# Banded attention scores from fp16 high and low parts, a later partial sum in each group, and other orders in two head loops

## The reference

```python
s = jnp.einsum('bnqhgd,bnkhd->bnhgqk', qb, kc).astype(jnp.float32) * (HEAD_DIM ** -0.5)
s = jnp.where(mask[None, :, None, None], s, NEG_INF)
p = sink_softmax(s, sinks).astype(v.dtype)
o = jnp.einsum('bnhgqk,bnkhd->bnqhgd', p, vc)
```

## Time and profile before

| | |
|---|---|
| median of 3 runs | 1790.39 us |
| profiled execution | 1791.63 us, of it 1790.0 us between first and last instruction |
| TensorE (PE) busy | 1734.6 us, 97% of the span |
| VectorE (DVE) busy | 1061.5 us, 59% |
| ScalarE (ACT) busy | 876.1 us, 49% |
| GpSimd (POOL) busy | 226.5 us, 13% |

### The profile page before, as it was taken

The page is one execution under the profiler, slowest core; times in us unless marked ns, Lnnn a source line. Parts: engine busy times, 40 slices in busy tenths (PEclk is TensorE's granted clock), DMA queues, the critical chain, the costliest instruction groups (busy, mean ns, idle before and its releaser), DMA issues.

```text
span 1790.0 us, 36899 instructions
## 1 busy us (share of the span) xinstructions
PE 1734.6 (97%) x14593; PEld 1356.9 (76%) x14593; DVE 1061.5 (59%) x2267; ACT 876.1 (49%) x1345; POOL 226.5 (13%) x313
## 2 busy tenths in 40 slices
PE   6999999999999999999999999999999999999996
PEld 4888876787677867786667777777777777778885
DVE  6634646574557546774766875555665666574343
ACT  7545542553345444553335664544655555464442
POOL 1410010111011001101105102011011100011110
PEclk8999999999999999999999999999999999999998
DMA  9523323552255225642455533233233323234432
GB/s 305 154 71 97 81 54 95 168 162 77 60 174 169 71 63 180 197 142 76 131 161 168 171 95 100 80 94 91 70 82 82 82 71 81 77 95 129 114 96 100
DMA packets 270549, 204.51 MB, mean 114 GB/s; under 512 B 8116, under 2 KB 254080, under 8 KB 269136
## 3 DMA queue, kind: packets, MB, share of 16 engines
q1 hardware_dynamic: 251200, 131.71, 26.7%
q0 software_dynamic: 19232, 71.13, 11.7%
HBM read 168.05 MB, written 38.80 MB: 116 GB/s over the span
## 4 chain that ended last, share of the span: by engine, by line
PE 81%; DVE 8%; ACT 5%; issue 3%; DMA 2%; SPq 0%; ACTq 0%; DVEq 0%; POOL 0%; POOLq 0%
PE PP L604 53%; PE PP L853 7%; PE PP L633 3%; PE BS L697 2%; PE BS L507 2%; PE B L1050 2%; PE BS L757 2%; PE B L728 2%; ACT W L1229 1%; PE B L507 1%; ACT AR L1602 1%; DVE W L1836 1%; PE PP L1143 1%; PE B L779 1%; DMA W<-in_w_out_a 1%
## 5 line engine op out<-in xcount | busy, mean ns | idle before, releaser
L604 PE MATMUL PP<-H,W 128*128 128x280 f16 (+1 forms) x8640 | 1053.4, 281 | 2.6 <-DVE W L1836 1.9
L604 PEld LDWEIGHTS PP<-H,W 128*128 128x128 f16 x8640 | 833.4, 98 | 189.6 <-issue 21.3
L1229 ACT ACTIVATE W<-W,SCL 128x1024 f16<-128x1024 f32 x240 | 262.6, 1138 | 312.3 <-DVE SCL L1767 271.5
L1836 DVE SCALAR_TENSOR_TENSOR W<-W,SCL 128x1024 f16<-128x1024 f32 x240 | 310.4, 1303 | 131.1 <-ACT W L1229 126.6
L1218 ACT ACTIVATE wjunk<-W 128x2048 bf16<-128x2048 f32 x120 | 227.7, 1898 | 16.4 <-DMA W<-in_w_out_a 12.0
L853 PE MATMUL PP<-O,W 128*128 128x280 f16 x1536 | 189.1, 283 | 4.1 <-DVE H L2094 2.7
L853 PEld LDWEIGHTS PP<-O,W 128*128 128x128 f16 x1536 | 147.4, 98 | 43.9 <-issue 8.5
L1602 ACT ACTIVATE AR<-AR 128x128 f32<-128x128 f32 x136 | 53.0, 391 | 90.6 <-DVE AR L2381 90.6
L604 PE MATMUL PP<-O,W 128*128 128x280 f16 x576 | 69.6, 283 | 0.5 <-DVE AR L2321 0.5
L2011 DVE SCALAR_TENSOR_TENSOR AR<-AR,B 128x512 f32<-128x512 f32 x32 | 23.9, 747 | 73.2 <-PE B L728 51.2
L1766 DVE TENSOR_SCALAR step<-PP 128x1 int32<-128x1 int32 x107 | 16.5, 154 | 83.8 <-PE PP L534 81.0
(11 more groups left out here) (352 smaller groups left out, 1861.7 us busy)
## 6 DMA issues: line engine op xcount, KB each, us to landing
W<-in_w_in_a SPq DMA_DIRECT2D x48, 1024.0 KB, 6.0
W<-in_w_in_b SPq DMA_DIRECT2D x32, 1024.0 KB, 6.0
out<-AR POOLq DMA_DIRECT2D x36, 512.0 KB, 4.3
AR<-in_state_gla POOLq DMA_DIRECT2D x32, 512.0 KB, 6.6
W<-in_w_out_b SPq DMA_DIRECT2D x16, 1024.0 KB, 6.1
W<-in_w_out_a SPq DMA_DIRECT2D x16, 512.0 KB, 5.3
W<-in_w_out_a SPq DMA_DIRECT2D x32, 256.0 KB, 3.9
W<-in_w_kv SPq DMA_DIRECT2D x8, 1024.0 KB, 5.6
```

The costliest lines, as they stand in the source:

```text
L604: last = mm(PP[j % 2][:, c, 0:cols], w[:, k, :], x[:, c * cols:(c + 1) * cols], start=s_, stop=e)
L1229: A(w_parts(j % 2)[0][:, ks], W[:, j % 2, ks], ACT.Copy, scale=SCL[:, j % 4, 0:1]).then_inc(w_hi, 1)
L1836: STT(out=low[:, ks], in0=W[:, j % 2, ks], scalar=SCL[:, j % 4, 0:1], in1=high[:, ks], op0=ALU.mult, op1=ALU.subtract).then_inc(w_ready, 1)
```

## The change

Five things change.

1. Banded scores. The keys and the query tiles are kept as two fp16 parts (`kp`, `qp`), and a score is three products of a 64 x 128 half of the array (`for x, y in ((0, 0), (0, 1), (1, 0))`), row halves 0 and 64 in turn, into B0 and B1. ACT writes the high parts (`group_q`, `key_high`), VectorE the low ones (`query_low`, `key_low`), and the PSUM buffer is now freed by VectorE. The factors that the parts leave go into the softmax (`QF`, `KF`). The sample queries keep an fp32 copy of 32 columns. GpSimd's copy into `kg` is gone.
2. In a group, the block sum that stands in unit j = 1 moves from the fifth tile to the eighth (`7 if j == 1 else 4`).
3. In the head loop, unit 1's scale comes before `distance` on VectorE, and its high part before `level_decay` on ACT.
4. In the last head, `outa_add` at q = 17 comes before `head_norm`.
5. In the last head, ACT cuts two tiles of O before it sums unit 13, and VectorE scales tiles 14 and 15 together, one step later.

```diff
@@ batch_scores
-                    for r in range(GRP):
-                        a = HD * (r % 2)
-                        q = qB[a:a + HD, r // 2, :]
-                        key = kg[a:a + HD, :]
-                        bank, c = (B0, B1)[r % 2], 2 * P * (r // 2)
-                        for s in range(2):
...
+                    for u in range(GRP // 2):
+                        c = 2 * P * u
+                        spans = ((c, slice((k - 1) * P, (k + 1) * P)),) if k else (
+                            (c + P - META, slice(SEQ + SMP, TOK)), (c + P, COLS[0]))
+                        for at, keys in spans:
+                            for x, y in ((0, 0), (0, 1), (1, 0)):
+                                for a, bank in ((0, B0), (HD, B1)):
+                                    last = mm(bank[:, at:at + keys.stop - keys.start], qp[a:a + HD, u, x, COLS[k]],
+                                              kp[a:a + HD, y, keys], start=(x + y == 0), stop=(x == 1), skip_group_check=True)
@@ group_piece
-                project(group_unit_at(i, j), j, j, SWA // 2 + 2 * i + 1, H, fresh, (a, b), after, HALF_B)
+                project(group_unit_at(i, j), j, j, SWA // 2 + 2 * i + 1, H, fresh, (a, b), after, HALF_B, 7 if j == 1 else 4)
@@ ACT head_step
+                    if rec and n == 0:
+                        unit_high(head_unit_at(h, 1), 1)
@@ ACT last_head
+                o_high(12, 13)
                 total(13)
-                o_high(12, 13, 14, 15)
+                o_high(14, 15)
@@ ACT group_q, key_high
-                A(halves(qB[:, j - 2, 0:LIVE]), PV(j, HALF_B), ACT.Copy, scale=unscale(j + 2)).then_inc(pp_free[j % 2], 1)
+                A(qB[:, j - 2, :], PP[j % 2][:, 1, SEQ - HALF_B:HALF_B], ACT.Copy, scale=unscale(j + 2))
+                A(halves(qp[:, j - 2, 0, :]), PV(j, HALF_B), ACT.Copy, scale=2.0 ** -SCORE_BITS).then_inc(parts_hi, 1)
+            def key_high(i):
+                if not first(i):
+                    act.wait_ge(sc_done, NB * i)
+                A(kp[:, 0, :], tile(kdup, i), ACT.Copy, scale=KF[:, 0, ds(i, 1)]).then_inc(parts_hi, 1)
@@ DVE, the K/V projection
+            def key_factors(j):
+                for g in (2 * j, 2 * j + 1):
+                    TS(KF[:, 0, g:g + 1].bitcast(I32), unscale(j).bitcast(I32), -1, 0x7F000000 - (SCORE_BITS << 23), ALU.mult, ALU.add)
+                    TS(KF[:, 1, g:g + 1], unscale(j), 2.0 ** (2 * SCORE_BITS) * HD ** -0.5, None, ALU.mult)
+            key_factors(0)
             kv_keep(0)
             unit_low(kv_unit_at(2), 2, (1,))
+            key_factors(1)
             kv_keep(1)
@@ DVE, groups
+            def query_low(i, j):
+                dve.wait_ge(parts_hi, 3 * (i + 1) + (j if first(i + 1) else 2 * j - 3))
+                STT(out=halves(qp[:, j - 2, 1, :]), in0=PV(j, HALF_B), scalar=2.0 ** -SCORE_BITS, in1=halves(qp[:, j - 2, 0, :]),
+                    op0=ALU.mult, op1=ALU.subtract).then_inc(pp_free[j % 2], 1)
...
+                if k < NT:
+                    for u in range(GRP // 2):
+                        of = slice(2 * u, 2 * u + 2)
+                        last = STT(out=nm[:, of], in0=m[:, of], scalar=QF[:, u:u + 1], in1=SK[:, ds(GRP * i + 2 * u, 2)],
+                                   op0=ALU.mult, op1=ALU.min)
...
+                TS(QF[:], SCL[:, 0:2, 1], KF[:, 1, ds(i, 1)], None, ALU.mult)
                 spread_q(i)
...
+                    if not last and n == 6:
+                        query_low(i, 2)
+                        key_low(i + 1)
...
+                    if not last and n == 7:
+                        query_low(i, 3)
@@ GpSimd stage
-                G.tensor_copy(kg, tile(kdup, i)).then_inc(kg_ready, 1)
```

More of the change, by code:

```diff
@@ L205, in yoco_kernel @@
         SKR = sb("SKR", [P, KV])
+        KF = sb("KF", [P, 2, KV])
+        QF = sb("QF", [P, 2])
         small = sb("small", [P, 72])
@@ L295, in yoco_kernel @@
         THb = take([2, TOK])
-        qB = take([2, TOK])
+        qB = take([2, SMP])
+        qp = take([2, LIVE]).bitcast(FP16).rearrange("p j (s n) -> p j s n", s=2)
         Cc, Pp = take([2, GRP * P]), take([2, GRP * P])
@@ L300, in yoco_kernel @@
         kcat = take([DB // 2, P + DT])
-        kg, vg, vxg, vmg = take([TOK]), take([NT, HD]), take([HD]), take([HD])
+        kp = take([TOK]).bitcast(FP16).rearrange("p (s n) -> p s n", s=2)
+        vg, vxg, vmg = take([NT, HD]), take([HD]), take([HD])
         sm = take([2, 32])
@@ L1404, in head_step @@
                         prepare_sum(head_unit_at, (h,), 5)
-                    if n % 2 == 0 and not (first(h) and n == 0):
+                    if n % 2 == 0 and n and not (first(h) and n == 0):
                         unit_high(head_unit_at(h, n // 2 + 1), n // 2 + 1, (1,) if first(h) and n == 2 else (0, 1))
@@ L1601, in batch_exp @@
                 for r in range(heads):
-                    A(Pp[:, b, r * P:(r + 1) * P], Cc[:, b, r * P:(r + 1) * P], ACT.Exp, scale=HD ** -0.5,
+                    A(Pp[:, b, r * P:(r + 1) * P], Cc[:, b, r * P:(r + 1) * P], ACT.Exp,
+                      scale=QF[:, r // 2:r // 2 + 1] if k < NT else HD ** -0.5,
                       bias=sm[:, b, 4 + r:5 + r], accum_out=sm[:, b, 16 + r:17 + r]).then_inc(sm_act, 1)
@@ L1648, in group_step @@
                     act.wait_ge(o_summed, i + 1)
+            act.wait_ge(setup, 8)
+            key_high(0)
             for j in (2, 3):
@@ L2095, in outa_add, with head_scores @@
                     op1=ALU.add).then_inc(pp_free[n % 2], 1)
-            def head_scores(i, n):
+            def head_scores(i, n, scale=None):
                 if n < 7:
@@ L2102, in head_scores @@
                     level_qk(i, n + 2)
+                if n == 0 and scale is not None:
+                    scale()
                 if n < 3:
@@ L2165, in prepare, with scale @@
                 def prepare(j, part):
-                    if part == 0:
-                        unit_scale(head_unit_at(h, j), j, 3 if split and j == U_HEAD else 0)
+                    if part == 0 and not (rec and j == 1):
+                        scale(j)
                     unit_low(head_unit_at(h, j), j, (part,))
+                def scale(j):
+                    unit_scale(head_unit_at(h, j), j, 3 if split and j == U_HEAD else 0)
                 if rec:
@@ L2174, in head_step @@
                     if rec:
-                        head_scores(i, n)
+                        head_scores(i, n, lambda: scale(1))
                     if first(h) and n in (3, 4):
@@ L2247, in last_head @@
                         outa_add(6 + q // 4, q % 4)
-                    if not (3 <= q < 7 or 16 <= q < 20):
+                    if q == 17:
+                        head_norm(i, NT)
+                    elif not (3 <= q < 7 or 16 <= q < 20):
                         head_seqs(i, q, 0)
@@ L2344, in _, with key_low @@
             dve.wait_ge(setup, 8)
+            def query_low(i, j):
+                dve.wait_ge(parts_hi, 3 * (i + 1) + (j if first(i + 1) else 2 * j - 3))
+                STT(out=halves(qp[:, j - 2, 1, :]), in0=PV(j, HALF_B), scalar=2.0 ** -SCORE_BITS, in1=halves(qp[:, j - 2, 0, :]),
+                    op0=ALU.mult, op1=ALU.subtract).then_inc(pp_free[j % 2], 1)
+            def key_low(i):
+                dve.wait_ge(parts_hi, 3 * i + (1 if first(i) else 2))
+                STT(out=kp[:, 1, :], in0=tile(kdup, i), scalar=KF[:, 0, ds(i, 1)], in1=kp[:, 0, :], op0=ALU.mult,
+                    op1=ALU.subtract)
             def spread_q(i):
@@ L2379, in batch_max @@
                 t.link(dve, V.tensor_reduce(m, x, AX.X, ALU.max, negate=True))
-                t.link(dve, STT(out=nm, in0=m, scalar=HD ** -0.5, in1=nsink, op0=ALU.mult, op1=ALU.min))
+                if k < NT:
[3 more added lines that the diff above has]
+                                   op0=ALU.mult, op1=ALU.min)
+                    t.link(dve, last)
+                else:
+                    t.link(dve, STT(out=nm, in0=m, scalar=HD ** -0.5, in1=nsink, op0=ALU.mult, op1=ALU.min))
                 t.link(dve, TT(d, nm, nsink, ALU.subtract))
@@ L2460, in group_step @@
                     dve.wait_ge(pp_free[b], 8 + SWA // 2 + 2 * i + 1)
+                if not first(i):
+                    dve.wait_ge(sm_act, (GRP * NT + 1) * i)
+                TS(QF[:], SCL[:, 0:2, 1], KF[:, 1, ds(i, 1)], None, ALU.mult)
                 spread_q(i)
```

29 lines of the change are left out of this document (12 added, 17 removed).

## The result

The changed kernel takes 1793.90 us (median of 14 runs, 1791.76 to 1797.86) against 1790.47 us before (14 runs, 1788.62 to 1793.65): a ratio of 1.0019, 95% interval 1.0012 to 1.0026, so it is slower by 3.4 us. The forecast was 1784.1 us, range 1778 to 1790. The profiled execution of the change took 1796.44 us, its span 1794.9.

The account below looks back on a forecast made before the run. TensorE was taken as the bound, except in the last group, bound by the VectorE/ScalarE chain. Terms -1.9 - 1.6 - 2.4 - 1.3 + 0.25 + 0.6 = -6.3 us gave 1785.3 profiled, 1784.1 median; range 1778 to 1790.

Parts of the forecast that it names:

- the one taken first: Whole kernel: TensorE sets the time, so VectorE or ScalarE instructions add 0 while TensorE's inputs come in time.
- The waits come back elsewhere: Rival: thin covers at unit 0's block sum and k = 0 scores fail, or VectorE late in last head; 1788 us, chance 0.22.
- Group waits at L539: Sign against the forecast: TensorE waits of 0.3 us reappearing in the groups at that line.
- Heads: Heads 1 to 3: unit 1's earlier scale and high part remove three TensorE waits for the low part, -1.9 us.
- Last head: Last head: earlier H update and two high parts first bring the last block forward, -1.6 us for both edits.
- Block sum: Groups: the later block sum no longer waits for the gate, 0.35 us in each of seven groups, -2.4 us.
- Scores: Banded scores in seven groups: fp16 blocks take 0.78 us instead of 0.82, block 0 0.82 instead of 0.89, -1.3 us.
- The third rival: Banded scores: halves pair better than quarters did, blocks 0.67 and block 0 0.6 us; total 1780 us, chance 0.14.
- Buffer later: Groups: VectorE's low part frees the PSUM buffer later, but covers of about 0.3 us hold, 0; otherwise +4 us.
- K/V: K/V projection: small factor instructions before kv_keep delay the block sum of j = 1, +0.25 us.
- Last group: Last group: VectorE's chain gets 0.1 us more in each of four blocks, cached keys come 0.15 us later, +0.6 us.
- Rival of the loads: Banded scores: a row half's weight loads do not hide behind its streams, +16.5 us in seven groups; 1802 us, chance 0.06.

Follow-up runs that it names:

- the orders alone: Kernel before with only the four order edits (block sum, heads, two in last head), scores left in fp32: 1786.0 us, ratio 0.9966.
- change_sumback: Changed kernel with the block sum of unit j = 1 moved back to the fifth tile: 1794.9 us, ratio 1.0017 to the kernel before.
- the further run: The changed kernel run once more, nothing altered: 1794.5 us, period 58.94 us; its last group took 41.75 us at a granted clock of 1.00.
- fixed_scale: Changed kernel with parts in true units: one constant scales all scores, maxima scaled in one instruction, K/V factors gone: 1783.4 us, ratio 0.9955 to before.
- before_column: Kernel before, but the exponential of the four banded blocks reads its scale from an SBUF column holding the same constant: 1798.9 us, ratio 1.0035.
- fixed_split: fixed_scale with VectorE's scaling of the maxima in two instructions, constants as scalars: 1783.1 us, ratio 0.9955 to the kernel before.

## Why the prediction was wrong

The step that failed is the one taken first: "an instruction added on VectorE or ScalarE costs nothing as long as what TensorE needs from it still comes in time". The rule is right, but it was then applied to the new instructions of the buffers alone ("So **0**"). The softmax of the steady groups has no term in the sum at all: by that rule its cost was put at nothing, without a look at the slack it would need. The split scaling was priced for the last group only, at 0.1 us a block, and the exponential's new operand was priced nowhere. What the runs showed in its place is 2.25 us more on the chain in a group, of which 1.6 come out in the period (58.97 against 57.36). The sum had a group gain 0.35 + 0.19 us, a period of 57.59; it became 58.97. Seven times the difference is 9.7 us. The forecast missed by 9.8 in the median; for the profiled execution (1796.44 against 1785.3) it missed by 11.1, and there the last group has 1.8 more.

The trace of before shows where this chain meets TensorE. At the first gate of a group it is late, seven times by 0.29 us. At the second gate it is early: ScalarE ends it at 1395.03, and TensorE's block sum stands at 1396.31, 1.28 us later:

```profile
1394.34 0.69 ACT L1291 ACTIVATE AR<-PP,SCL 128x544 f32<-128x544 f32 x1
1396.31 0.17 PE L534 MATMUL PP<-WSUM,ones 128*128 128x1 bf16 x1
```

The prediction read the first as a wait to be removed by asking later, and did not look at the second. With the wait removed TensorE comes there 0.35 us sooner, and some 0.1 us pass between a gate and the block sum that waits for it, so about 0.8 us of slack were left for 2.25 us more on the chain. That is an estimate of 1.4 us a group, from rows that were at hand, beside the 1.38 us by which the period missed its forecast. "The waits come back elsewhere" was the rival nearest to it, but with other places (the block sum of unit 0, block 0's scores), which stayed free of waits in the seven groups, and with +4 us. Group waits at L539 were among the signs that the prediction named for being wrong; they came, at the third block sum of a group, and three times as long.

Term by term:
- *Heads* (-1.9): right. No wait of the earlier trace rows is left in the heads:

```profile
194.56 1.89 PE L702 MATMUL BS<-AR 128*128 128x64 f32 x16
196.30 3.02 PE L609 MATMUL PP<-H,W 128*128 128x280 f16 x24
```

- *Last head* (-1.6): right. The waits of the earlier trace rows from 926 to 949 us and the 0.21 us between their last two, 3.42 us in all, became 0.89, 0.23 and 0.47, so -1.8; the 0.9 us left at the sample product was forecast:

```profile
929.44 0.39 PE L805 MATMUL B<-AR 32*128 32x512 bf16 x2 [0.89 <-DVE AR L2077]
...
944.17 0.89 PE L858 MATMUL PP<-O,W 128*128 128x280 f16 x6 [0.23 <-DVE O L1855]
945.53 2.32 PE L858 MATMUL PP<-O,W 128*128 128x280 f16 x18 [0.47 <-DVE O L1855]
```

- *Block sum* (-2.4): right as a term by itself (period 58.13 to 57.79 with the orders alone, 7 x 0.34 = 2.4), and worth nothing beside the longer chain (change_sumback).
- *Scores* (-1.3): right in sign, too small. With a free chain the period falls by 0.43 us (57.79 to 57.36), 3.0 us in seven groups; a block took 0.76 and not 0.78, block 0 0.60 and not 0.82. The third rival (the halves pair better) had block 0 right, with 0.6 us, and the other blocks, with 0.67, too small.
- *Buffer later* (0): right, no wait at the block sum of unit 0 or at block 0 in the seven groups.
- *K/V* (+0.25): no wait appeared at the block sum of 1031.30, so 0.
- *Last group* (+0.6): +2.4 in the profiled execution, 1.9 in the further run at the higher clock. The prediction named the chain as the bound there, but gave it 0.1 us more in a block; the exponentials and the scalings add 0.37 + 0.19, in four blocks 2.2 us.
- *Rival of the loads*: wrong, as expected. In a block the loads of the weights lie like this:

```profile
1371.48 0.55 PEld L1008 LDWEIGHTS BS<-AR 64*128 64x128 f16 x12 [0.22 <-issue]
```

Each load has 94 ns in the median, six to a row half; with six streams of 0.111 us (the estimate of the prediction) behind them they would be 1.23 us a block, where 0.76 passed. The rule of the Trainium skill (TensorE: Matmul & The Clock Gate, "Part 3: Packing small matmuls — row/col tiling"), by which a load overlaps only a matmul in another row group, does not agree with that.

fixed_scale, which has all of the change but the longer chain, came to 1783.4 us: the forecast was that of a kernel whose softmax has not changed. That it lies so near 1784.1 is in part luck: it is 8.5 us below the kernel before run beside it (1791.9), where 6.3 were forecast, as the scores gained more than their term.

## What to carry to other kernels

Before pricing a change by the busiest engine, measure the slack of the other engines' chain at each place where the busy one meets it: a wait of 0.3 us there, however short, says that the slack at that place is zero, and that an instruction added to the chain ahead of it costs its full time. Where the busy engine comes later than what it needs, the distance in time is the slack, and only what goes beyond it costs anything. Compare not only which instructions a change adds but in which form the old ones now stand: a constant that becomes a column makes every exponential dearer. A moved wait is a gain only if the engine that ends it has time to spare.

## What the runs showed of the hardware

- An exponential of 128 x 128 on ScalarE, its bias in a column, takes 390 ns with a constant scale (fixed_scale; 391 in the kernel before) and 483 with its scale in a column as well (the change; 482 in before_column).
- On VectorE, too: a scaling of 128 x 2 takes 157 ns with a constant scalar (fixed_split) and 219 with one from a column (the change).
- Twelve fp16 matmuls of 256 columns, in turn in the two row halves, pass in 0.76 us with twelve loads of 94 ns, and 24 smaller ones of block 0 in 0.60 us.
